# Layer 2's modulation vectors in a two-layer hybrid backbone: four of six weighed on VectorE in layer 1's feed-forward

## The reference, cut to what matters

```python
for l in range(DEPTH):
    sh1, sc1, g1, sh2, sc2, g2 = _modulation(c, mod_w[l], mod_b[l], 6)
    h = _rmsnorm(x, norm1_w[l]) * (1.0 + sc1) + sh1
    y, yc = _token_mixer(h, hc, ...)
    x = x + g1 * y
    h2 = _rmsnorm(x, norm2_w[l]) * (1.0 + sc2) + sh2
    x = x + g2 * _conv_ffn(h2, ffn_up[l], ffn_conv_w[l], ffn_conv_b[l], ffn_down[l])
def _conv_ffn(h, w_up, conv_w, conv_b, w_down):
    a, b = jnp.split(h @ w_up, 2, axis=-1)
    return (jax.nn.silu(_dwconv(a, conv_w) + conv_b) * b) @ w_down
```

## Time and profile before

| | |
|---|---|
| median of 3 runs | 2840.16 us |
| profiled execution, its own time | 2843.68 us |
| its span | 2841.9 us |
| granted TensorE clock, mean | 0.994 |
| PE busy | 2754.6 us, 97% |
| DVE busy | 1270.0 us, 45% |
| ACT busy | 1009.2 us, 36% |
| POOL busy | 1114.8 us, 39% |
| mean transfer rate | 88 GB/s |

### The profile page before, as it was taken

One profiled execution on the slowest core, in us unless ns is written; L12 is line 12 of the kernel. 1 busy time (PEld: TensorE's weight loads), 2 busy tenths in 40 slices (PEclk: granted clock), 3 DMA queues, 4 the chain that ended last, 5 costly groups with the idle time before them and its releaser, 6 DMA issues. The chain is left out here.

```text
span 2841.9 us, 44189 instructions
## 1 busy us (share of the span) xinstructions
PE 2754.6 (97%) x17420; PEld 2390.0 (84%) x17420; DVE 1270.0 (45%) x2803; ACT 1009.2 (36%) x1894; POOL 1114.8 (39%) x976
## 2 busy tenths in 40 slices
PE   7999999999999999999999989999999999999998
PEld 4888888899998898888888878877888888888887
DVE  4555437524453035332333555645725441344446
ACT  4333227533332225222232353334733332433332
POOL 2333331153333333433433443433154345465555
PEclk9999999999999999999999999999999999999999
DMA  6111220022223133212112231222023222532233
GB/s 240 60 60 60 69 88 24 16 93 90 90 75 119 60 149 116 84 56 72 60 60 74 104 123 57 75 89 82 16 100 110 84 75 80 202 104 89 89 104 111
DMA packets 39371, 249.55 MB, mean 88 GB/s; under 512 B 4480, under 2 KB 4864, under 8 KB 13568
## 3 DMA queue, kind: packets, MB, share of 16 engines
q1 hardware_dynamic: 36288, 236.25, 23.7%
q10 hardware_dynamic: 2880, 10.49, 0.9%
HBM read 236.23 MB, written 10.49 MB: 87 GB/s over the span
## 5 line engine op out<-in xcount | busy, mean ns | idle before, releaser
L2381 POOL TENSOR_TENSOR w_rest<-raw,w_head 128x512 fp32r<-128x512 f32 (+1 forms) x634 | 833.0, 1345 | 899.6 <-ACT w_head L1413 890.4
L971 PE MATMUL psum_products<-h_head,w_head 128*128 128x512 f32 (+2 forms) x2288 | 820.0, 358 | 4.8 <-DVE h_rest L1860 2.2
L971 PE MATMUL psum_products<-h_rest,w_head 128*128 128x512 f32 (+2 forms) x2288 | 802.4, 351 | 0.0
L971 PE MATMUL psum_products<-h_head,w_rest 128*128 128x512 f32 (+2 forms) x2288 | 801.4, 350 | 0.0
L971 PEld LDWEIGHTS psum_products<-h_head,w_head 128*128 128x128 f32 (+1 forms) x2288 | 428.2, 187 | 66.0 <-DVE h_rest L1860 3.4
L971 PEld LDWEIGHTS psum_products<-h_rest,w_head 128*128 128x128 f32 (+1 forms) x2288 | 427.7, 187 | 63.6 <-issue 0.9
L971 PEld LDWEIGHTS psum_products<-h_head,w_rest 128*128 128x128 f32 (+1 forms) x2288 | 428.7, 187 | 56.9 <-issue 1.5
L1413 ACT ACTIVATE w_head<-raw 128x1024 fp32r<-128x1024 f32 (+1 forms) x321 | 320.4, 1044 | 400.7 <-PE psum_products L971 343.3
L971 PE MATMUL psum_products<-w_head,h_head 128*128 128x256 f32 x1408 | 403.9, 287 | 1.6 <-DVE h_rest L1920 1.6
L971 PE MATMUL psum_products<-w_rest,h_head 128*128 128x256 f32 x1408 | 392.0, 278 | 0.0
L971 PE MATMUL psum_products<-w_head,h_rest 128*128 128x256 f32 x1408 | 391.8, 278 | 0.0
(11 more groups left out here) (291 smaller groups left out, 3795.5 us busy)
## 6 DMA issues: line engine op xcount, KB each, us to landing
raw<-in_stream SPq DMA_DIRECT2D x184, 1024.0 KB, 4.9
raw<-in_stream SPq DMA_DIRECT2D x16, 512.0 KB, 3.6
mods_mid<-in_stream SPq DMA_DIRECT2D x8, 1024.0 KB, 10.5
residual<-stage ACTq DMA_DIRECT2D x16, 512.0 KB, 2.6
stage<-residual SPq DMA_DIRECT2D x14, 512.0 KB, 4.9
mods_b<-in_stream SPq DMA_DIRECT2D x5, 1024.0 KB, 24.0
mods_a<-in_stream SPq DMA_DIRECT2D x3, 1024.0 KB, 14.1
x_in<-in_x SPq DMA_DIRECT2D x4, 512.0 KB, 9.0
```

Of the source, the lines that this page charges most:

```text
L971: return nc.tensor.matmul(o, a, b, start=start, stop=stop)
L2381: G.tensor_tensor(wl[:, s["sp"] % 2, a:b], place_of(s)[:, a:b], wh[:, s["sp"] % 2, a:b].bitcast(F32), ALU.subtract).then_inc(*ev.mark("poo ...
```

## The change

Sixteen slots, the vectors 1, 2, 3 and 4 of layer 2, leave the places where `vectors` handed them out (two in retention and two in the feed-forward of layer 1, three at its end, nine in layer 2's mlstm and retention). A new generator `hosted(16)` puts one of them behind each `up` of layer 1, u = 1 to 16. There the step `msum` has DVE multiply the quarter's two k-tiles by two columns of `csilu` into `macc` (`mod_weighed`, two rows of 128x1024), four instructions of 128x1024 a slot, and it is DVE's last one that releases the slot. When four quarters are in, `mod_sums` sums over the partitions on PE with a matrix of ones (8 matmuls of 32x256 a vector), DVE makes `vrow` from it, and `columns` follows as before. Vector 0 and vector 5 keep their four slots each in the norms.

```diff
+    def hosted(count):
+
+        turn, before, ready = None, None, None
+        for l, v, part in islice(modulation, count):
+            s = slot(l, ("mod_w", 2 * part * P, [(v * D, D)]), 2, False)
+            if ready is not None:
+                turn = step("mod_sums", prev_v=before, **ready)
+                before, ready = ready["v"], None
+            made[0] += part == 0
+            step("msum", s, l=l, v=v, quarter=part, prev_v=before)
+            yield
+            if part == 1 and turn is not None:
+                step("columns", l=l, v=turn["v"], g=turn["g"], mixer=True)["bank"] = None
+                turn = None
+            if part == 3:
+                ready = dict(l=l, v=v, g=made[0] - 1)
...
@@ mlstm
-            if ctx or hd + 1 == MH:
+            if ctx:
...
-                late, first_q = vectors(2), aq_pieces(s)
+                late, first_q = vectors(2) if ctx else iter(()), aq_pieces(s)
...
@@ retention
-            count_v = (3, 3, 2, 4)[hd] if ctx else (2, 2, 1, 1)[hd]
-            more, last = vectors(count_v), len(tiles) + 1
-            more_now = 2 * count_v if hd + 1 < RH else 4 if ctx else 2
+            count_v = (3, 3, 2, 2)[hd] if ctx else 0
+            more, last = vectors(count_v) if ctx else iter(()), len(tiles) + 1
+            more_now = 2 * count_v
...
@@ feed-forward, after each up
-                more = vectors(2, mixer=True) if ctx else iter(())
+                more = hosted(16) if ctx else iter(())
...
-                for _ in islice(more, (0, 1, 2, 1)[u] if u < 4 else 0):
+                for _ in islice(more, 1):
                     pass
...
@@ end of the layer
-        fill = iter(()) if last else vectors(3)
-        for _ in islice(fill, 3):
-            pass
...
@@ TensorE
+                elif kind == "mod_sums":
+                    for row in range(2):
+                        pe.wait_ge(*ev.at("msum", l, st["v"], KD - 1, row))
...
+                    for row in range(2):
+                        for q in range(4):
+                            last = mm(psm[32 * q:32 * q + 32, 4, row * COLS:(row + 1) * COLS], c("ones")[:, 0:32],
+                                      macc[:, row, q * COLS:(q + 1) * COLS])
...
@@ VectorE
+                elif kind == "msum":
+                    dve.wait_ge(*ev.at("raw", s["n"]))
...
+                            if k == 0:
+                                V.tensor_scalar(macc[:, row, :], w[:, 0, :], weight, None, ALU.mult).then_inc(
+                                    *ev.mark("dve", "msum", l, v, k, row))
+                            else:
+                                dve.wait_ge(*ev.at("msum", l, v, k - 1, row))
+                                V.scalar_tensor_tensor(out=macc[:, row, :], in0=w[:, k % 2, :], scalar=weight,
+                                                       in1=macc[:, row, :], op0=ALU.mult, op1=ALU.add).then_inc(
+                                    *ev.mark("dve", "msum", l, v, k, row))
+                    ev.now[("raw_free", s["n"])] = {"dve": ev.count["dve"]}
```

More of the change, by code:

```diff
@@ L298, in make_plan @@
             if hd + 1 == MH:
-                late, first_q = vectors(2), aq_pieces(s)
+                late, first_q = vectors(2) if ctx else iter(()), aq_pieces(s)
                 plan.append(dict(kind="split", slot=s))
                 more = 2 if ctx else 4
-                pieces, fill = pieces + 2 + more, chain(fill, islice(late, 2), islice(first_q, more))
+                pieces, fill = pieces + 2 * ctx + more, chain(fill, islice(late, 2), islice(first_q, more))
                 ticks("mtiles", len(tiles), fill, pieces * len(tiles) // count, stop=len(tiles), l=l, hd=hd, tiles=tiles)
@@ L442, in make_plan @@
         step("region", name="mlp")
+        for _ in fill if ctx else ():
+            pass
         step("up_early", s, 0, l=l, gen=gen, u=0, ctx=ctx, half=1, open=True)["bank"] = first["bank"]
@@ L478, in make_plan @@
             step("down", ends[half], 1, l=l, u0=18, kt=4, items=[(tiles[k], half)],
-                 open=0 < i < len(items) - 1)
+                 open=i > 0 and not (last and i == len(items) - 1))
             k = {2: 0, 3: 1, 5: 2}.get(i) if last else i // 2 - 1 if i >= 2 and i % 2 == 0 else None
@@ L482, in make_plan @@
                 step("norms", ticks=range(k, k + 1), **norm)
-        fill = iter(()) if last else vectors(3)
-        for _ in islice(fill, 3):
-            pass
         step("norms", ticks=range(n - 1, n), **norm)
-        for _ in fill:
-            pass
         if not last:
@@ L676, in backbone @@
         bias_b = Region()("bias_b", [P, D])
+        macc = Region()("mod_weighed", [P, 2, D])
         R = Region()
@@ L1058, in _ @@
                 l, hd, t = st.get("l"), st.get("hd"), st.get("t")
-                if kind == "split":
+                if kind in ("split", "msum"):
                     continue
@@ L1102, in _ @@
                     last.then_inc(*ev.mark("pe", "rows", l, st["v"], st["quarter"]))
+                elif kind == "mod_sums":
+                    for row in range(2):
+                        pe.wait_ge(*ev.at("msum", l, st["v"], KD - 1, row))
+                    if st["prev_v"] is not None:
+                        pe.wait_ge(*ev.at("vec", l, 4 * st["prev_v"] + 3))
+                    for row in range(2):
+                        for q in range(4):
+                            last = mm(psm[32 * q:32 * q + 32, 4, row * COLS:(row + 1) * COLS], c("ones")[:, 0:32],
+                                      macc[:, row, q * COLS:(q + 1) * COLS])
+                    last.then_inc(*ev.mark("pe", "mod_sums", l, st["v"]))
                 elif kind == "columns":
@@ L1819, in _ @@
                         ev.now[("rows_sb", l, st["v"], part)] = {"dve": ev.count["dve"]}
+                elif kind == "msum":
+                    dve.wait_ge(*ev.at("raw", s["n"]))
+                    w, v = raw_of(s), st["v"]
+                    if st["quarter"] == 0 and st["prev_v"] is not None:
+                        dve.wait_ge(*ev.at("mod_sums", l, st["prev_v"]))
+                    for k in range(2 * st["quarter"], 2 * st["quarter"] + 2):
+                        for row in range(2):
+                            weight = csilu[:, k, row:row + 1]
+                            if k == 0:
[7 more added lines that the diff above has]
+                    ev.now[("raw_free", s["n"])] = {"dve": ev.count["dve"]}
+                elif kind == "mod_sums":
+                    row = vrow[:, st["g"] % 2, :]
+                    dve.wait_ge(*ev.at("mod_sums", l, st["v"]))
+                    dve.wait_ge(*ev.at("vturn", st["g"] - 2))
+                    V.tensor_scalar(row, psm[:, 4, 0:COLS], c("pick")[:, 0:1], None, ALU.mult).then_inc(
+                        *ev.mark("dve", "row", l, st["v"]))
+                    dve.wait_ge(*ev.at("row", l, st["v"]))
+                    V.scalar_tensor_tensor(out=row, in0=psm[:, 4, COLS:2 * COLS], scalar=c("pick")[:, 1:2], in1=row,
+                                           op0=ALU.mult, op1=ALU.add).then_inc(*ev.mark("dve", "rows_sb", l, st["v"], 3))
                 elif kind == "columns":
```

## The result

The changed kernel takes 2978.57 us (median of 4 runs, 2977.04 to 2981.4) against 2840.27 us for the kernel before (4 runs, 2839.01 to 2843.3). The ratio is 1.0486, with a 95% interval of 1.0468 to 1.0505: 138 us slower. The forecast was 2979 us in 2930 to 3015.

A forecast was written before the change was run, and what follows sets the result against it. TensorE, busy 97% of the span, was taken to bound the kernel. The terms 120.8 + 8 + 4 - 2.6 + 20.4 - 12 gave +138.6 us on 2843.7, or 2979 us after 3.5 us of profile offset; range 2930 to 3015.

The forecast's parts named there:

- The loop through the ring: Layer 1's feed-forward: VectorE's late slot release delays up load, split and bank copies; 26.95 us against a 16.64 us period.
- second load landed after the release: In each turn of layer 1's feed-forward, modulation load then up load land 9.57 us after the release.
- `msum`: VectorE's four instructions in each turn take 5.7 us, bounds 5.1 to 7.4; 5.0 for a vector's first slot.
- clock, each of twelve: TensorE's granted clock falls behind each of twelve waits, 1.7 us each, 20.4 in all; bounds 0 and about 2 each.
- twelve turns with their clock: Layer 1's feed-forward: twelve paying u cost 8 x 10.3 + 4 x 9.6 = 120.8 us, plus 20.4 for the clock.
- four downs: At u = 4, 8, 12, 16 `msum` delays copies into `acc`; TensorE waits about 2 us each, 8 us.
- the stage: Layer 1's feed-forward, where the sixteen slots are placed, grows by about 150 us.
- everywhere else: Fourteen slots leaving layer 2, layer 1's retention and layer 1's end save 12 us; the three at that end save nothing.
- two loads land together: Rival, in the loop: both loads land in 4.9 us instead of 9.57, 56 us less, 2923 us; chance 0.10.
- held up by POOL: Rival, on VectorE: all four `msum` instructions take 1.85 us, 20 us more, 2999 us; chance 0.12.
- No clock loss: Rival: the loop is right but TensorE keeps its clock, 20 us less, 2959 us; chance 0.15.
- Not slower: Rival: VectorE's 5.41 us gap takes `msum` and loads run far enough ahead, 2830 to 2838 us; chance 0.05.

The follow-up runs named there:

- swapped loads: Against the changed kernel, SP loads the up slot following a modulation slot ahead of that modulation slot; 2849.91 us, ratio to the kernel before 1.004.
- filler: Changed kernel plus nine TensorE matmuls on constants, results unread, in eleven of the twelve waits; 2955.46 us, ratio to the kernel before 1.0408.
- early `msum`: Changed kernel with `msum` moved between the convolution's taps and the gate, and `mod_sums` ahead of the next `up`; 2870.38 us, ratio to the kernel before 1.0101.
- a quarter of the work: Changed kernel with three of four `msum` instructions left out in quarters 1 to 3 of each vector; 2921.74 us, ratio to the kernel before 1.0296.

## Why the prediction was right, point by point

**The loop through the ring** was the step on which all rested, and it held. Twelve waits before the last bank, at u = 2 to 4, 6 to 8, 10 to 12 and 14 to 16, none at u = 5, 9 and 13, periods of 27.6 to 28.3 us for a predicted 27 to 29. TensorE's waits were 6.7 to 9.5 us long for a predicted 10 or so, and the clock behind them made up for part of it. Swapping two loads takes away some 127 us, and releasing the same slots from TensorE takes away the waits too, while shortening VectorE's work does not come near that. So this cause is shown and not only argued.

**Its terms** were less exact than their sum. Those that were off, with what was measured:

| term | predicted | measured |
|---|---|---|
| second load landed after the release | 9.57 | 7.38 (1160.75 to 1168.13), 7.3 to 8.4 over the twelve |
| `msum` | 5.7 | 6.48 |
| clock, each of twelve | 1.7 | 27.1 / 12 = 2.3 |
| twelve turns with their clock | 120.8 + 20.4 = 141.2 | 98.0 + 27.1 = 125.1 |
| four downs | 8 | 4 x 2.38 + 3 x 1.7 = 14.6 |
| the stage | 150.6 | 145.8, of which these terms, four `mod_sums` and two `rows` less give 141.4 |
| everywhere else | -12 | -9 |

The largest miss is the loads. The 9.57 came from the one place of before that was read for it, and it is longer than any of the twelve in the change. The kernel with `rows` in this place needs 7.4 too (1141.65 to 1149.07). The rival "two loads land together" had the direction right and about half of its size. The second miss works the other way. At the downs I priced the wait (2 us, measured 2.38) and no clock behind it. I had taken the full clock behind the 0.62 us wait for a sign that short waits are free. At 2.4 us they mostly are not. Behind the twelve waits the clock's 2.3 us each lies above my bound of about 2 as well. The two sums, -16 and +7, cancel in part, and with 4.4 us of the stage that these terms don't account for it came out within 5 us. Most of the 4.4 lies in the twelve turns: their periods add up to 333.5 us, which less 12 x 16.64, 1.75 for the late gates in u = 2 (18.39 - 16.64 with the swapped loads) and three `mod_sums` of 1.1 is 128.8, against the 125.1 of waits and clock. The other places then missed by 3 the other way. That the forecast of 2979 met 2978.57 so closely is luck; the mechanism and the size of the loop are not.

**`msum`** was predicted between 5.1 and 7.4, with POOL's `u_rest` as the only company. The tile's list shows what happened:

```profile
L1862 DVE SCALAR_TENSOR_TENSOR mod_weighed<-raw,c_silu,mod_weighed x56: 1271/1274/2900, 1130.0 to 1624.7; 128x1024 f32<-128x1024 f32 x56
```

Most instructions take 1.27 us, the duration that the earlier trace rows gave, and the one that meets `u_rest` takes up to 2.90. The Trainium skill (SBUF — State Buffer, Who interferes with whom) has VectorE with two SBUF inputs and a reading GpSimd instruction shut each other out for a whole instruction, and by it I had said that one `msum` instruction could wait out `u_rest`, up to 1.9 us. The trace agrees: 2.90 - 1.27 = 1.6. The rival "held up by POOL" named a price of 7.4 for all four, and did not occur: when `msum` runs, POOL has only `u_rest` to do, as the reason given against it said.

**The clock** fell behind all twelve waits, and behind three of the four at the downs. The Trainium skill (TensorE: Matmul & The Clock Gate, HAM oscillation) describes just that, waits for data that send the clock down before each tile. The trace agrees twelve times out of twelve for the waits of 6.7 to 9.5 us, and the filler matmuls show a cost of at least 23 us. "No clock loss" is refuted.

**Elsewhere.** Layer 1's end and layer 2's mlstm together gave 3.1 us, for three slots each, 0.5 of it by the last `xs` copy of layer 1. Layer 2's retention gave 4.6 for six and layer 1's retention 1.8 for two (the changes of the offset between the same `xs` and `a_s` copies of the two traces). That is 0.8 to 1 us a slot, a little less than taken, and next to nothing for the three at the end of layer 1, as taken. Most of the miss of 3 us is in layer 2's retention, 4.6 for a predicted 6.8; why was not tested.

**The profile's own offset.** I took 3.5 us off because before's profiled execution stood above its median. The two traces show where it lay: at the first `a_s` copy, ahead of every moved instruction, the change is already 3.6 us earlier. It was a difference between two executions, at their start, and belonged out of the sum.

**"Not slower"** had named its deciding point: the up load not standing behind the modulation load that `msum` releases, for 2830 to 2838 us. The swapped loads make that case, and measured 2849.91. The mechanism was right. Of the 12 us above its upper figure some 7 are the downs, 14.6 for the 8 priced. Most of the rest is in the other places: by the traces they gave back 6.4 us in this kernel, for the 12 taken; why less than the 9 of the change was not tested.

## What to carry to other kernels

When work moves from the bounding engine to one with spare time, ask first what that work releases, and which queue stands behind the release; the spare time says nothing of it. Here an engine 46% busy held a load queue for 463 us, and the repair was the order of two loads. Read a period off the timeline and add up one turn of the loop: with the clock it gave 28.65 us for turns of 27.6 to 28.3, although its terms were off by 2 and 1 in opposite ways. And before the work is moved, ask what it costs where it is: leaving it out altogether was worth 0.4%, and the move put 4.9% at risk.

## What the runs showed of the hardware

The clock answers to short waits, but not to every one. Of four waits of 2.38 us three brought the lower level, 1.7 us lost each, in the change, with the swapped loads and with the filler alike. With the early `msum`, the wait of 3.29 us at 1176.13 cost 1.7 us in the two stretches behind it (0.65 and 0.93), while behind the one of 3.57 us at 1284.70 the clock stayed at 1.00. In the kernel with a quarter of the work, eight waits of 3.4 to 5.0 us cost 2.2 us each behind them, four of 7.1 to 7.8 us the same 2.2, and in the change twelve of 6.7 to 9.5 us cost 2.3 each. So the number of such waits counts as well as their length, and a kernel with 87 us of useless matmuls in them was 23 us faster.

VectorE and POOL beside each other gain little over taking turns. With the loads swapped, `u_rest`, four pieces of `w_rest` and four `msum` instructions together lasted from 1143.11 to 1154.47, 11.4 us. One behind the other they would take 1.87 + 5.4 (POOL's four pieces in before, from 1254.91 on) + 4.87 = 12.1. A median scalar_tensor_tensor of 128x1024 took 2.33 us in place of 1.27, as the tile's list of that kernel has it:

```profile
L1868 DVE SCALAR_TENSOR_TENSOR mod_weighed<-raw,c_silu,mod_weighed x56: 1272/2328/2903, 1129.8 to 1495.6; 128x1024 f32<-128x1024 f32 x56
```

Putting VectorE's part at a place where POOL is idle, between taps and gate, brought it to 4.87.

One thing wasn't tried: homes outside the ring for the modulation slots, which would free the up loads from `msum` in another way than the swap.
